# Neighbourhood attention: query tiles of 16 columns by 8 rows, and the position bias as an identity product

## The reference, cut to what matters

```python
col_start = jnp.clip(col - NA_WIN_COLS // 2, 0, GRID_W - NA_WIN_COLS)
col_in = (col[None, :] >= col_start[:, None]) & (col[None, :] < col_start[:, None] + NA_WIN_COLS)
...
s_loc = jnp.einsum('bqhd,bkhd->bhqk', q_r, k_b).astype(jnp.float32) * scale + bias
s_loc = jnp.where(band_mask, s_loc, NEG_INF)
s_ctx = jnp.einsum('bqhd,bchd->bhqc', q_r, k_ctx).astype(jnp.float32) * scale
p = jax.nn.softmax(jnp.concatenate([s_loc, s_ctx], axis=-1), axis=-1).astype(v.dtype)
```

## Time and profile before

| | us |
|---|---|
| median of 3 runs | 4004.82 |
| their spread | 4001.94 to 4045.99 |
| the profiled execution | 4024.9 |
| its span on the core | 4023.2 |
| TensorE busy in the span | 3653.6 |
| mean granted clock of TensorE | 0.924 |

### The profile page before, as it was taken

One profiled execution on the slowest core, in us unless ns is written; L12 is line 12 of the kernel. 1 busy time (PEld: TensorE's weight loads), 2 busy tenths in 40 slices (PEclk: granted clock), 3 DMA queues, 4 the chain that ended last, 5 costly groups with the idle time before them and its releaser, 6 DMA issues. The chain is left out here.

```text
span 4023.2 us, 38545 instructions
## 1 busy us (share of the span) xinstructions
PE 3653.6 (91%) x14286; PEld 1996.4 (50%) x14286; DVE 1555.2 (39%) x2687; ACT 924.7 (23%) x1425; POOL 643.3 (16%) x388
## 2 busy tenths in 40 slices
PE   7999989889989999989999895665899999999998
PEld 6844447454455854446754442553344444444443
DVE  4223463316233220002221299997424424423522
ACT  1002025213341011113301231223223212312311
POOL 4600000000003610002101131663001001100100
PEclk9999978999999999995589998787899999999999
DMA  3212110143322221120011331335434334323422
GB/s 134 84 63 84 63 63 0 42 167 114 137 100 73 94 74 52 65 87 27 11 42 63 112 150 73 125 141 188 152 120 141 115 109 151 136 103 127 146 104 83
DMA packets 93926, 393.65 MB, mean 98 GB/s; under 512 B 3728, under 2 KB 69392, under 8 KB 71312
## 3 DMA queue, kind: packets, MB, share of 16 engines
q1 hardware_dynamic: 21744, 302.85, 20.5%
q10 hardware_dynamic: 70944, 85.46, 6.2%
q0 software_dynamic: 1152, 4.19, 0.3%
HBM read 348.45 MB, written 44.04 MB: 98 GB/s over the span
## 5 line engine op out<-in xcount | busy, mean ns | idle before, releaser
L742 PE MATMUL bank<-work 128*128 128x512 bf16 x2048 | 784.8, 383 | 63.8 <-DVE work L1926 38.6
L743 PE MATMUL bank<-work 128*128 128x512 bf16 x2048 | 784.8, 383 | 0.0
L744 PE MATMUL bank<-work 128*128 128x512 bf16 x2048 | 784.5, 383 | 0.0
L742 PEld LDWEIGHTS bank<-work 128*128 128x128 bf16 x2048 | 201.1, 98 | 323.8 <-issue 41.6
L1208 ACT ACTIVATE work<-ring 128x4096 bf16<-128x4096 f32 x65 | 234.9, 3615 | 517.3 <-PE bank L744 467.6
L617 PE MATMUL bank<-hF,ring 128*128 128x512 f32 x768 | 336.0, 600 | 12.4 <-ACT hF L928 11.6
L1915 DVE TENSOR_TENSOR work<-ring,work 128x4096 bf16<-128x4096 f32 x57 | 252.2, 4425 | 199.5 <-ACT work L1208 183.3
L744 PEld LDWEIGHTS bank<-work 128*128 128x128 bf16 x2048 | 202.2, 99 | 247.2 <-issue 9.8
L743 PEld LDWEIGHTS bank<-work 128*128 128x128 bf16 x2048 | 201.9, 99 | 239.9 <-issue 3.6
L1898 DVE TENSOR_TENSOR work<-const,work 128x2048 f32<-128x2048 f32 x64 | 246.8, 3931 | 3.6 <-ACTq L165 3.6
L728 PE MATMUL bank<-work 128*128 128x128 f32 x1024 | 157.2, 326 | 99.3 <-POOL work L2115 99.3
(11 more groups left out here) (247 smaller groups left out, 4485.1 us busy)
## 6 DMA issues: line engine op xcount, KB each, us to landing
ring<-in_wstream SPq DMA_DIRECT2D x142, 2048.0 KB, 7.7
gates<-work ACTq DMA_DIRECT2D x16, 2048.0 KB, 6.3
work<-gates ACTq DMA_DIRECT2D x32, 1024.0 KB, 6.3
hidden<-hF ACTq DMA_DIRECT2D x8, 1024.0 KB, 3.9
hF<-hidden ACTq DMA_DIRECT2D x8, 1024.0 KB, 8.6
work<-in_rpb POOLq DMA_DIRECT2D x8, 512.0 KB, 3.8
xF<-in_x SPq DMA_DIRECT2D x1, 2048.0 KB, 7.5
out<-hF SPq DMA_DIRECT2D x4, 512.0 KB, 2.7
```

What stands on the lines that cost most here:

```text
L742: pe.matmul(out, a(0), b(0), start=(k == 0), stop=False)
L743: pe.matmul(out, a(0), b(1), start=False, stop=False)
L744: mm = pe.matmul(out, a(1), b(0), start=False, stop=(k == n - 1))
```

## The change

A query tile becomes 16 grid columns by 8 rows. Its window then lies in 32 columns, so it needs 8 x 32 = 256 of the 512 grid keys, and together with the 256 context keys a tile has one bank of 512 scores. Queries are stored in tile order (`D_QF`), keys are read with a strided pattern straight from `D_KF`, and the copies by POOL go. The bias is not added by DVE: TensorE writes it into the bank as the product of the identity with the bias tile, and the scores are accumulated on top. One maximum, one exponential, one copy of 512 elements a tile. The pipeline is three deep, and the loops are written out.

The bias tiles have to be gathered from the table: `arrange_bias()` on ACT copies 192 pieces, DRAM to DRAM, 16 x 8 runs of 32 floats each. The values are needed in tile order too: POOL stores them to DRAM and gathers them by 32 transfers of 32 rows. The mask comes by 24 transfers. The outputs are put back into grid order by the copies behind `turn_branches()` (`by_grid`).

```diff
+        def by_grid(k):
+
+            if k >= 4:
+                return hF[:, k, :], bank[:, k, :]
+            return (hF[:, k, :].rearrange("p (r t c) -> p t r c", r=8, t=NT),
+                    bank[:, k, :].rearrange("p (t r c) -> p t r c", t=NT, r=8))
...
+        KEY_COL = [0, 8, 24, 32]
+        BIAS_OF = [0, 1, 1, 2]
...
+                def scores(n):
+                    h, qt = n // NT, n % NT
+                    half = slice(64 * (h % 2), 64 * (h % 2) + 64)
+                    q = D_QF[half, h // 2, qt * P:(qt + 1) * P]
+                    near = D_KF[half, h // 2, 0:S].rearrange("p (r c) -> p r c", r=8)
+                    if n >= 3:
+                        pe.wait_ge(weighed, n - 2)
                     if qt == 0:
...
+                        pe.wait_ge(signal("n_bias"), h + 1)
+                    pe.matmul(bank[:, n % 3, 0:256], ident, D_BIAS[:, h % 2, BIAS_OF[qt], 0:256],
+                              start=True, stop=False)
+                    pe.matmul(bank[:, n % 3, 0:256].rearrange("p (r c) -> p r c", r=8), q,
+                              near[:, :, KEY_COL[qt]:KEY_COL[qt] + 32], start=False, stop=True)
+                    pe.matmul(bank[:, n % 3, 256:512], q, D_KF[half, h // 2, S:S + CTX],
                               start=True, stop=True).then_inc(scored, 1)
...
+                    tiles = (2 * qt, 2 * qt + 1, 8, 9)
...
+                scores(0)
+                scores(1)
+                for n in range(last):
+                    if n + 2 < last:
+                        scores(n + 2)
+                    turn(n)
+                    if n >= 2:
+                        values(n - 2)
+                values(last - 2)
+                values(last - 1)
                 meet()
...
+            def arrange_bias():
+
+                for v in range(3):
+                    qc, kc = (0, 16, 48)[v], (0, 8, 32)[v]
+                    for r in range(8):
+                        for h in range(NA_HEADS):
+                            near = rpb_d[h, qc:qc + 16, (7 - r) * 64:(15 - r) * 64].rearrange(
+                                "p (k c) -> p k c", c=64)[:, :, kc:kc + 32]
+                            act.dma_start(rpb_tiles[h, v, 16 * r:16 * r + 16, :].rearrange("p (k c) -> p k c", c=32),
+                                          near).then_inc(signal("n_rpb_arranged"), 16)
...
+                    act.activation(D_P[:, n % 3, :], bank[:, n % 3, :], ACT.Exp, scale=0.125,
...
             norm("a0")
             conv_in("a_in0")
+            arrange_bias()
             norm("b")
...
+                    dve.wait_ge(scored, n + 1)
+                    order(v.reduce_max(st[:, 0, qt:qt + 1], bank[:, n % 3, :], AX))
...
+                def load_bias(h):
+                    for v in range(3):
+                        pool.dma_start(D_BIAS[:, h % 2, v, 0:256], rpb_tiles[h, v]).then_inc(rpb_in, 16)
+
+                pool.wait_ge(signal("d_q_taken"), 18)
+                pool.dma_start(v_rows.rearrange("(t p) n -> p t n", p=P), D_VR).then_inc(operands, 16)
+                for v in range(3):
+                    qc, kc = (0, 16, 48)[v], CONST["colmask"][0] + (0, 8, 32)[v]
+                    for r in range(8):
+                        pool.dma_start(D_MASK[16 * r:16 * r + 16, v, :], const_d[qc:qc + 16, kc:kc + 32])\
+                            .then_inc(operands, 16)
+                for u in range(2):
+                    g.memset(D_BIAS[:, u, :, 256:512], 0.0)
+                pool.wait_ge(signal("n_rpb_arranged"), 192 * 16)
+                load_bias(0)
+                pool.wait_ge(operands, 25 * 16)
+                rows_ = v_rows.rearrange("(r c) n -> r c n", r=8)
+                for qt in range(NT):
+                    for r in range(8):
+                        part = 32 * (r % 4)
+                        pool.dma_start(D_V[part:part + 32, 2 * qt + r // 4, :],
+                                       rows_[r, KEY_COL[qt]:KEY_COL[qt] + 32, :]).then_inc(operands, 16)
+                for h in range(NA_HEADS):
+                    pool.wait_ge(rpb_in, 3 * 16 * (h + 1))
+                    for v in range(3):
+                        b = D_BIAS[:, h % 2, v, 0:256].rearrange("p (k c) -> p k c", c=32)
+                        ins = g.tensor_tensor(b, b, D_MASK[:, v, :].rearrange("p (a c) -> p a c", a=1)
+                                              .broadcast_to([P, 8, 32]), ALU.add)
+                    order(ins)
+                    g.tensor_scalar(D_BIAS[:, h % 2, :, 0:256], D_BIAS[:, h % 2, :, 0:256], 8.0, None, ALU.mult)\
+                        .then_inc(bias_made, 1)
+                    if h + 1 < NA_HEADS:
+                        if h >= 1:
+                            pool.wait_ge(signal("n_scored"), NT * h)
+                        load_bias(h + 1)
                 meet()
```

More of the change, by code:

```diff
@@ new lines, in turn, with values @@
+                def turn(n):
+                    pe.wait_ge(weighed, n + 1)
+                    if n >= 3:
+                        pe.wait_ge(moved, n - 2)
+                    for kt in range(4):
+                        mm = pe.transpose(bank[:, 3 + n % 3, kt * P:(kt + 1) * P],
+                                          D_P[:, n % 3, kt * P:(kt + 1) * P], ident)
+                    mm.then_inc(turned, 1)
+                def values(n):
+                    h, qt = n // NT, n % NT
+                    pe.wait_ge(moved, n + 1)
+                    if n == 0:
+                        pe.wait_ge(signal("n_operands_in"), 57 * 16)
+                    if qt == 0 and h >= 2:
@@ L661, in values @@
                         pe.wait_ge(taken, h - 1)
-                    for kt in range(6):
-                        mm = pe.matmul(bank[:, 6 + u, qt * 64:(qt + 1) * 64], D_PT[:, qt % 2, kt * P:(kt + 1) * P],
-                                       D_V[:, kt, ds(h * 64, 64)], start=(kt == 0), stop=(kt == 5))
+                    tiles = (2 * qt, 2 * qt + 1, 8, 9)
+                    for j, kt in enumerate(tiles):
+                        mm = pe.matmul(bank[:, 6 + h % 2, qt * 64:(qt + 1) * 64], D_PT[:, n % 3, j * P:(j + 1) * P],
+                                       D_V[:, kt, h * 64:h * 64 + 64], start=(j == 0), stop=(j == 3))
@@ L665, in values @@
                     mm.then_inc(summed, 1)
[L667 to L691, removed]
@@ L692, in neighbourhood @@
-                pair(3, closing=True)
-                values(NA_HEADS - 1, 1, NT - 1, False)
+                last = NT * NA_HEADS
+                scores(0)
[8 more added lines that the diff above has]
+                values(last - 1)
                 meet()
@@ L1134, in in_takes @@
             def in_takes():
-                out = [(0, j == 3, D_QF[:, j, :], ACT.Copy) for j in range(4)]
+                out = [(0, j == 3, D_QF[:, j, :].rearrange("p (t r c) -> p t r c", t=NT, r=8), ACT.Copy)
+                       for j in range(4)]
                 out += [(1, False, D_KF[:, j, 0:S], ACT.Copy) for j in range(4)]
                 out += [(1, j == 3, D_KF[:, j, S:S + CTX], ACT.Copy) for j in range(4)]
-                out += [(2, t == 5, D_V[:, t, :], ACT.Copy) for t in range(6)]
+                out += [(2, False, D_VR[:, t, :], ACT.Copy) for t in range(NT)]
+                out += [(2, t == 1, D_V[:, 8 + t, :], ACT.Copy) for t in range(2)]
                 for m, dst in ((3, D_GU), (4, D_GV)):
@@ L1158, in move @@
[L1158 to L1171, removed]
@@ L1187, in neighbourhood @@
+                last = NT * NA_HEADS
+                exps(0)
+                exps(1)
+                for n in range(last):
+                    move(n)
+                    if n + 2 < last:
+                        exps(n + 2)
                 meet()
@@ L1782, in neighbourhood @@
-                with dve.Fori(1, 3) as i:
-                    order.n = base + 20 * (i - 1)
-                    pair(i)
-                order.n = base + 40
-                pair(3, closing=True)
-                finish(7, 1)
+                for n in range(NT * NA_HEADS):
+                    if n >= 2 * NT and n % NT == 0:
+                        finish(n // NT - 2)
+                    bias(n)
+                finish(NA_HEADS - 2)
+                finish(NA_HEADS - 1)
                 meet()
```

167 lines of the change are left out of this document (45 added, 122 removed).

## The result

| | before | after |
|---|---|---|
| median, us | 4011.46 (4 runs) | 4083.98 (4 runs) |
| spread, us | 4001.94 to 4045.99 | 4078.29 to 4091.56 |
| span of the profiled execution, us | 4023.2 | 4076.5 |
| mean granted clock | 0.924 | 0.921 |

The account below looks back on a forecast made before the run. TensorE at the low clock was taken to bound the stage: 47.2 + 8 + 92.0 + 2 = 149.2 us against 231.6, -82.4, with +38.5 for the arrangement, -43.9. Forecast 3961 us, 8-in-10 range 3925 to 4065.

Parts of the forecast that it names:

- Part 1: Bias table arrangement on ACT before the norm: 192 transfers at 0.45 us, 86.4 us of queue, delaying the norm by 38.5 us.
- The rival of slow pieces: Arrangement's small DMA pieces drain slowly and hold ACT: 4039 us at full clock, 4115 at low clock; chance 0.12.
- Part 2: POOL's work behind the meeting before the first bias: 60 issues at 0.70 us plus sums and scaling, 47.2 us.
- Part 3: TensorE's work for one new query tile: 5.51 us at the low clock, 3.01 us at the full clock.
- Part 4: Clock in the rewritten stage: starts low after the pause, then rises after 8 us, a guess.
- the clock stays low: Rival: the rewritten stage never leaves the low clock and takes 225.5 us, 4037 us in all; chance 0.20.
- The 60 us of the first attention: Wait at low clock before the rise there; as a late rise in the changed stage it gave 3984 us, chance 0.13.

Follow-up runs that it names:

- e10: Changed kernel with bias tiles laid out by the host, plus 192 ACT loads of 16 rows of 1 KB into SBUF and a wait for landing: 4031.15 us.
- e2: Changed kernel with the same 192 ACT issues, each carrying 16 runs of 1 KB instead of 128 runs of 128 bytes: 4082.64 us.
- e3: Changed kernel with 24 ACT issues instead of 192, each for all eight heads with 128 runs of 1 KB: 4005.93 us.
- e4: Changed kernel with POOL's preparation and the bias of heads 0 and 1 moved ahead of the meeting: 3966.55 us, ratio 0.9882 to the kernel before.
- e6: Changed kernel with all 128 rows instead of 64 in the two products of queries and keys: 3988.51 us.
- e1: Changed kernel with bias tiles laid out by the host, without the 192 ACT transfers: 4006.65 us, ratio 0.9963 to the kernel before.
- e8: Changed kernel with host-laid bias tiles and POOL's preparation ahead of the meeting, both at once: 3884.75 us, ratio 0.9675 to the kernel before.
- e7: Changed kernel with five added identity products of 512 columns on TensorE after the wait for the first bias: 3991.42 us.
- e9: Kernel before with POOL's two heads early, plus five identity products of 512 columns between first scores and first transposes: 3909.66 us.
- e5: Kernel before with POOL's copies and bias table for heads 0 and 1 moved ahead of the meeting: 4021.8 us.

## Why the prediction was wrong

**Part 1: the step that failed is the price of an issue.** The path was right: ACT's queue holds the squares, what lies past the first 48 us counts one to one, the squares start behind the last issue, and the last sum of DVE ends 9.4 us later (337.74 to 347.16; 9.5 forecast). With the measured 127.2 us for 192 x 0.45 = 86.4, that sum gives +79.3, and +80.3 was measured. The issue cost 0.66 and not 0.45. It goes from DRAM to DRAM; my rows were loads into SBUF, and e10 prices such a load of this size at 0.49. 0.66 lay inside my bounds, but I took a value near the cheap end although its row was of another kind. The rival of slow pieces also foretold a loss (4115 us with the low clock), but by another mechanism, and e2 and e3 rule that out: there was no full queue to begin with, since the first three issues already took 0.66 each (1.98 us).

**Part 2: right in kind, dear by 11.5 us.** TensorE waited for POOL's bias 35.7 us past the entry, not 47.2: the mask pieces took 0.48 us an issue, the gathers 0.49, the bias loads 0.55 (0.70 forecast, from a load of 128 rows at 0.61 and an allowance for dispatch of which the rows show nothing). No score of a later head waited for a bias.

**Part 3: right.** 5.61 us a tile at the low clock (5.51 forecast), 2.97 at the full one in e4 (3.01).

**Part 4: the step that failed, and the one that set the sign.** I took two rises elsewhere, at 630 and at 2030 us, as evidence that this mix would raise a low clock within 8 us. In the profiled execution of the kernel after it stayed low for 175 us, until 6 us behind the last score product, and by their mean clock of 0.918 to 0.921 the same holds for all four of its runs. The stage thus followed the rival "the clock stays low": 225.5 us less the 11.5 of part 2 is 214.0, measured 213.7. (That it fits so closely is partly luck: 32 tiles at 5.61 instead of 5.51 cost 3.2 us more, and the end of the stage was cheaper than forecast.) I had named the evidence that should have weighed more: the stage before, with 64-row products in 2.85 of a tile's 6.88 us, had not risen in 210 us. By the same terms the new tile had 1.96 of 5.51 us in such products, 36% after 41%: nearly the mix that had never raised the clock. I had counted only the tile's full-height products with the identity, 1.81 of 5.51 us, left out that the products with the values have full height too, and had no row that says how much of them is enough. e6 shows that the 64-row products matter: with full height in them the clock rose some 4 us behind the first product. The Trainium skill (TensorE: Matmul & The Clock Gate, Part 1) says that sustained activity releases the clock; here the engine's records were without a gap for 175 us at 0.50, so "busy" in a profile isn't what decides it.

The height of the operands isn't the whole rule either, as the ends of the two stages show. In the kernel after, the last score product was over at 2073.1 and the clock rose at 2079, among transposes and products with the values, all of full height. In the kernel before, the same two kinds of work ran alone from 2014 to 2027, and the clock stayed low:

```profile
2014.00:2027.00 13.00, 12.71 (x60) 12.52 (x60) 1.86 (x8) 3.01 (x8) 0.00 (x0) 0.50 0.00 0
```

Nor is it the same in every execution of the new tiles: e3 and e10 had the rise at this same place, e1 and e2 ended the stage without one. What sets them apart stays open.

**The waiting time at the low clock is no constant either.** The 60 us of the first attention, which I used as a bound, came from one execution (the clock rose at 630.7 there, not at 630.4). With the same code behind the same pause of 12.4 us the clock rose 17 to 22 us behind the entry in e8 (entry 568.82) and 87 to 92 us behind it in e1 (568.09); one row of TensorE and two stretches of e8:

```profile
585.25 1.68 PE L496 MATMUL bank<-const,work 128*64 128x128 f32 x8
```

```profile
580.00:585.00 5.00, 5.00 (x20) 4.01 (x21) 1.04 (x6) 2.33 (x7) 0.00 (x0) 0.50 0.01 3
585.00:590.00 5.00, 5.00 (x25) 3.21 (x25) 1.23 (x5) 2.57 (x7) 0.74 (x2) 0.85 0.00 0
```

The same of e1:

```profile
654.02 1.91 PE L496 MATMUL bank<-const,work 128*64 128x128 f32 x8
```

```profile
650.00:655.00 5.00, 5.00 (x22) 4.09 (x22) 0.64 (x4) 1.95 (x6) 0.00 (x0) 0.50 0.00 0
655.00:660.00 5.00, 5.00 (x25) 2.98 (x24) 2.07 (x8) 2.55 (x6) 0.74 (x2) 0.90 0.00 0
```

The wait is not arbitrary. In all twelve profiled executions the rise came 1.3 to 2.1 us behind the start of one and the same piece of work, the series of eight transposes that each head of this attention has every 13.9 us (L485 before, L496 after). Which head it was differed: 18 us behind the entry (e7, e8, e10), 32 (after, e2, e4, e6), 46 (e3, e9), 60 (before), 74 (e5) or 88 (e1). At half clock 70 us of waiting are 35 us of time. I take this for the larger part of the spread of every kernel here (some 20 us to each side), which was not tested by itself. It is also why the runs of one execution (e2, e3, e5, e6, e7, e9, e10) are read from their rows and stretches and not from their total.

**The range** (3925 to 4065) missed by 19 us. It took in the low clock at an issue of 0.45, and the dear issue at the full clock, but not both together: 4037 + 41 = 4078.

## What to carry to other kernels

Before counting what a change saves on TensorE, look for what it puts ahead of TensorE's first product, in every queue: here 60 POOL issues and the sums behind them, all behind a meeting, held it 36 us and 192 ACT issues ahead of a norm 80 us. Moving either away turned the loss into a small gain (0.4% in e1, 1.2% in e4), and moving both gave 3.3%. A stage with many products of half the rows can run at either clock nearly from end to end, as this one did, and what decided here was the clock at its start; keep TensorE without a gap over the start, by a deeper pipeline or a few idle full-height products, before anything else: that was worth 82 us where the better tiling was worth 21. Price an issue by a row of the same queue and the same two ends of the transfer; a row of another kind gives a bound and not the value.

## What the runs showed of the hardware

- An ACT issue of a transfer from DRAM to DRAM took 0.65 to 0.66 us with 128 pieces of 128 bytes, with 16 of 1 KB and with 128 of 1 KB; from DRAM into SBUF, with 16 of 1 KB, 0.49; from SBUF into DRAM, in the kernel before, 0.34 (L1262).
- A POOL issue of 16 or 32 rows took 0.48 to 0.50 us, one of 128 rows 0.54 (bias loads, kernel after) to 0.61 (kernel before) in the median.
- The clock fell from 1.00 to 0.50 after a gap of 3.1 us in TensorE's records (e5, with 64-row products ahead of it) and then stayed there for the stage, although the records after it had no gap. A long gap is not needed: in the kernel after it fell again at 2082.6, after a gap of 0.63 us, while e4 kept 1.00 over the same gap at 1964.54.
- The same tiles ran at 2.97 or at 5.61 us each, from the first tile to the last, by the clock at which they were entered.
- A float32 product of 256 columns with 128 rows took no longer than one with 64: 0.59 us for the pair of records of the grid scores in e6, 0.70 in e4; the whole tile took 2.63 us in e6 (1915.28 to 1917.91), 0.34 less than in e4.
